# A second copy of the normalised tokens, ordered by remainder, for the values of two attention groups

## The reference

```
h = rmsnorm(x, mix_pre_norm)
z = h @ w_in
qa, ka, va, ... = split(z)
for g, (window, dil) in enumerate(((128, 1), (512, 4), (2048, 16))):
    o, lse = dilated_group_attention(qa[:, :, g], ka[:, :, g], va[:, :, g], bias[:, g], window, dil)
```

## Time and profile before

| | |
|---|---|
| median of 3 runs | 1440.94 us (1440.66 to 1441.42) |
| profiled execution | 1441.15 us, span in the trace 1439.0 us |
| granted TensorE clock | 0.999 of 2.4 GHz over the span |
| PE busy | 1431.7 us (99%) |
| PEld busy | 1227.9 us (85%) |
| DVE, ACT, POOL busy | 903.7 us (63%), 669.4 us (47%), 23.3 us (2%) |
| values, second and third group | from 376.93 to 424.12 us of the span |

### The profile page before, as it was taken

How to read it: one execution, slowest core, us unless ns; L and a number is a source line. 1 busy time by engine, 2 the same in 40 slices (tenths; PEclk the granted TensorE clock), 3 DMA queues, 4 the chain that set the end, 5 groups by cost and what they waited for, 6 DMA issues and landing times.

```text
span 1439.0 us, 21208 instructions
## 1 busy us (share of the span) xinstructions
PE 1431.7 (99%) x8104; PEld 1227.9 (85%) x8104; DVE 903.7 (63%) x1424; ACT 669.4 (47%) x1083; POOL 23.3 (2%) x43
## 2 busy tenths in 40 slices
PE   9999999999999999999999999999999999999998
PEld 8899999888898888888888888888889888888886
DVE  7888875335753455567866766664548555564975
ACT  5455555334532546555446554553445333233542
POOL 0000000000100000000000000000000000000000
PEclk9999999999999999999999999999999999999999
DMA  5333223324333323225322122224331243324653
GB/s 198 118 118 114 93 89 118 132 90 130 96 110 89 92 74 89 63 74 169 115 97 74 59 87 63 69 72 129 106 103 45 88 148 101 97 92 143 218 182 130
DMA packets 44317, 153.71 MB, mean 107 GB/s; under 512 B 5287, under 2 KB 5287, under 8 KB 44240
## 3 DMA queue, kind: packets, MB, share of 16 engines
q1 hardware_dynamic: 41472, 143.67, 31.3%
q0 software_dynamic: 2624, 8.95, 2.0%
q10 hardware_dynamic: 144, 0.04, 0.0%
HBM read 147.63 MB, written 4.23 MB: 106 GB/s over the span
## 4 chain that ended last, share of the span: by engine, by line
PE 98%; ACT 1%; DVE 1%; issue 0%; DVEq 0%; ACTq 0%
PE ps L470 21%; PE ps L471 21%; PE ps L472 21%; PE ps L637 4%; PE ps L638 4%; PE ps L639 4%; PE ps L1701 3%; PE ps L1700 3%; PE ps L1702 3%; PE ps L2530 1%; PE ps L2100 1%; PE ps L2101 1%; PE ps L2102 1%; PE ps L2913 1%; PE ps L2510 1%; PE ps L2933 1%
## 5 line engine op out<-in xcount | busy, mean ns | idle before, releaser
L470 PE MATMUL ps<-hh,whi 128*128 128x512 f32 x960 | 379.2, 395 | 0.1
L472 PE MATMUL ps<-hh,wlo 128*128 128x512 f32 x960 | 374.0, 390 | 0.0
L471 PE MATMUL ps<-hl,whi 128*128 128x512 f32 x960 | 373.9, 389 | 0.0
L416 DVE TENSOR_TENSOR wlo<-raw,whi 128x1024 fp32r<-128x1024 f32 x172 | 210.5, 1224 | 250.4 <-ACT whi L411 250.3
L411 ACT ACTIVATE whi<-raw 128x1024 fp32r<-128x1024 f32 x172 | 181.8, 1057 | 380.9 <-PE ps L472 356.3
L470 PEld LDWEIGHTS ps<-hh,whi 128*128 128x128 f32 x960 | 180.1, 188 | 42.6 <-issue 3.2
L472 PEld LDWEIGHTS ps<-hh,wlo 128*128 128x128 f32 x960 | 180.2, 188 | 38.1
L471 PEld LDWEIGHTS ps<-hl,whi 128*128 128x128 f32 x960 | 180.3, 188 | 35.7
L470 PE MATMUL ps<-ah,whi 128*128 128x512 f32 (+1 forms) x192 | 71.5, 372 | 0.0
L472 PE MATMUL ps<-ah,wlo 128*128 128x512 f32 (+1 forms) x192 | 71.3, 371 | 0.0
L471 PE MATMUL ps<-al,whi 128*128 128x512 f32 (+1 forms) x192 | 71.3, 371 | 0.0
(11 more groups left out here) (576 smaller groups left out, 3007.4 us busy)
## 6 DMA issues: line engine op xcount, KB each, us to landing
raw<-in_wstream SPq DMA_DIRECT2D x189, 512.0 KB, 3.5
w_raw<-in_wstream SPq DMA_DIRECT2D x32, 512.0 KB, 4.3
ring<-in_wstream SPq DMA_DIRECT2D x20, 512.0 KB, 4.3
xt<-in_x_t SPq DMA_DIRECT2D x16, 256.0 KB, 4.3
raw_early<-in_wstream SPq DMA_DIRECT2D x8, 512.0 KB, 4.4
raw_late<-in_wstream SPq DMA_DIRECT2D x4, 512.0 KB, 3.9
x_dram<-x_tok POOLq DMA_DIRECT2D x4, 512.0 KB, 4.1
x_tok<-x_dram POOLq DMA_DIRECT2D x4, 512.0 KB, 5.8
```

The lines of the kernel that those rows point to most:

```text
L416: nc.vector.tensor_tensor(wlo[:, s, :], raw[:, s, :], whi[:, s, :].bitcast(F32), ALU.subtract).then_inc(split_done, 1)
L470: nc.tensor.matmul(out, w, m, start=start, stop=False)
L471: nc.tensor.matmul(out, w, ml, start=False, stop=False)
L472: return nc.tensor.matmul(out, wl, m, start=False, stop=stop)
```

## The change

The change gives the second and third groups a stationary operand whose elements lie side by side.

- Sixteen new tiles, `hp_high0` to `7` and `hp_low0` to `7`, each [128, 4, 128]: the tokens of one `kt`, sorted by remainder. They lie in places that are used by others at other times: six of the high parts and the last two in the places of the attention's first `q_t` and `k_t`, the low parts where `whi_v` was and where `ath` and `atl` come later.
- POOL fills them for the second group: eight copies of `hh`, each when its tile is complete in both halves, then eight of `hl`, once PE is done with `whi_v`. PE waits for them tile by tile in the second group (`h_turned`).
- The normalised tokens are written straight into these tiles: DVE's `h_norm` reads `xt` and `rstd` in the order of the remainders and writes `tmp` in that order, ACT and DVE fill `hp_high` and `hp_low` from it.
- Later stages need the tokens' own order, so POOL copies each finished normalised tile back into `hh` and `hl`: 16 copies, after the bias transfers of the first two head pairs and ahead of the shift of the values. PE waits for all of them before the attention.
- Three transfers at the start count on one semaphore (`tables_in`) in place of two, so that ACT's wait at `table_h` and PE's waits for the constants are now for all three.

```
+        by_rest = "p (u r) -> p r u"
+        at[0] = arena + 51 * 1024
+        hp_high = [place(f"hp_high{i}", [P, R, U], F32R) for i in range(6)]
+        at[0] = arena + 68 * 1024
+        hp_high += [place(f"hp_high{i}", [P, R, U], F32R) for i in range(6, KT)]
+        at[0] = arena + 4 * S * (2 * FT + 1) + 4 * (2 * VEC + 3 * 32)
+        hp_low = [place(f"hp_low{i}", [P, R, U], F32R) for i in range(KT)]
...
-                        if t == 0 and g == 2:
-                            pe.wait_ge(sem("h_low"), IN_H + kt + 1)
+                        if t == 0:
+                            pe.wait_ge(*((sem("h_turned"), KT + kt + 1) if g == 1 else (sem("h_low"), IN_H + kt + 1)))
...
-                        m = [x[:, kt, :].rearrange("p (u r) -> p r u", r=R)[:, t, :] for x in (hh, hl)]
+                        m = hp_high[kt][:, t, :], hp_low[kt][:, t, :]
...
-                nc.scalar.activation(hh[:, d, :], tmp[:, d % 2, :], ACT.Copy).then_inc(sem("h_high"), 1)
+                nc.scalar.activation(hp_high[d][:].rearrange("p r u -> p (r u)"), tmp[:, d % 2, :], ACT.Copy
+                                     ).then_inc(sem("h_high"), 1)
...
-                nc.vector.scalar_tensor_tensor(out=tmp[:, d % 2, :], in0=xt[:, d, :], scalar=PRE2[:, d:d + 1],
-                                               in1=rstd[:], op0=ALU.mult, op1=ALU.mult).then_inc(sem("h_norm"), 1)
+                nc.vector.scalar_tensor_tensor(out=tmp[:, d % 2, :].rearrange("p (r u) -> p r u", r=R),
+                                               in0=xt[:, d, :].rearrange(by_rest, r=R), scalar=PRE2[:, d:d + 1],
+                                               in1=rstd[:].rearrange(by_rest, r=R), op0=ALU.mult, op1=ALU.mult
+                                               ).then_inc(sem("h_norm"), 1)
...
-                nc.vector.tensor_tensor(hl[:, d, :], tmp[:, d % 2, :], hh[:, d, :].bitcast(F32),
-                                        ALU.subtract).then_inc(sem("h_low"), 1)
+                nc.vector.tensor_tensor(hp_low[d][:].rearrange("p r u -> p (r u)"), tmp[:, d % 2, :],
+                                        hp_high[d][:].rearrange("p r u -> p (r u)").bitcast(F32), ALU.subtract
+                                        ).then_inc(sem("h_low"), 1)
...
+            for kt in range(KT):
+                pool.wait_ge(*counted("pre2", "ready", KT + kt + 1))
+                nc.gpsimd.tensor_copy(hp_high[kt][:], hh[:, kt, :].rearrange(by_rest, r=R)).then_inc(sem("h_turned"), 1)
+            pool.wait_ge(block_done, 2 * FIRST["v"] + 2)
+            for kt in range(KT):
+                nc.gpsimd.tensor_copy(hp_low[kt][:], hl[:, kt, :].rearrange(by_rest, r=R)).then_inc(sem("h_turned"), 1)
             pool.wait_ge(sem("vec_out"), 2)
             pool.dma_start(vec_dram.ap(), vec_sb[:]).then_inc(sem("pool_stored"), 16)
...
                     if hp == 2:
-
+                        pool.wait_ge(sem("h_turned"), 2 * KT)
+                        for d in range(KT):
+                            pool.wait_ge(sem("h_low"), IN_H + d + 1)
+                            for x, turned in ((hh, hp_high[d]), (hl, hp_low[d])):
+                                nc.gpsimd.tensor_copy(x[:, d, :].rearrange(by_rest, r=R), turned[:]
+                                                      ).then_inc(sem("h_turned"), 1)
                         pool.wait_ge(sem("v_scaled"), R)
...
             v_pe(pe)
             pe.wait_ge(sem("v_out0"), 2 * N_GROUPS + 1)
-            pe.wait_ge(sem("cst_in"), 16)
+            pe.wait_ge(sem("tables_in"), 48)
+            pe.wait_ge(sem("h_turned"), 4 * KT)
             attn_pe(pe)
```

More of the change, by code:

```diff
@@ L3297, in _ @@
             pool.wait_ge(sem(f"place_in{KT - 1}"), 16)
-            pool.dma_start(table[0:BUCKETS, :], rel_bias).then_inc(sem("hot_in"), 16)
-            pool.dma_start(hot_sb[:], onehot).then_inc(sem("hot_in"), 16)
-            pool.dma_start(cst[:], consts).then_inc(sem("cst_in"), 16)
+            pool.dma_start(table[0:BUCKETS, :], rel_bias).then_inc(sem("tables_in"), 16)
+            pool.dma_start(hot_sb[:], onehot).then_inc(sem("tables_in"), 16)
+            pool.dma_start(cst[:], consts).then_inc(sem("tables_in"), 16)
+            for kt in range(KT):
[4 more added lines that the diff above has]
+                nc.gpsimd.tensor_copy(hp_low[kt][:], hl[:, kt, :].rearrange(by_rest, r=R)).then_inc(sem("h_turned"), 1)
             pool.wait_ge(sem("vec_out"), 2)
@@ L3372, in _ @@
             nc.scalar.activation(lb_e[:], lb_e[:], ACT.Exp).then_inc(sem("lb_exp"), 1)
-            act.wait_ge(sem("hot_in"), 32)
+            act.wait_ge(sem("tables_in"), 48)
             act.wait_ge(sem("filled"), 1)
```

## The result

| | before | with the change |
|---|---|---|
| median | 1441.10 us (1440.66 to 1441.42, 4 runs) | 1458.86 us (1458.51 to 1460.08, 4 runs) |
| span in the trace | 1439.0 us | 1457.0 us |

The change makes the kernel slower: 17.8 us, a ratio of 1.0124 with a 95% interval of 1.011 to 1.0138. The forecast was 1452, its range 1441 to 1460.

A forecast was written before the change was run, and what follows sets the result against it. PE, busy 1431.7 of 1439.0 us, was taken as the bound. From 1441.15: less 1.6 for steps, plus 4.4 (first group's second half), plus 8.5 (second group's) gives 1452.4, forecast 1452, range 1441 to 1460.

The forecast's parts named there:

- PE's steps: Values' second and third groups: 192 matmul steps fall from 234.9 ns to 232.4 to 226.7, gaining 1.6 us (0.5 to 1.6).
- second half of the first group, first low copy: Seven copies at 0.85 us make DVE's last tile 3.7 us late, the first low part 0.7 more: 4.4 us.
- second half of the second group: DVE's chain to the last bank: six strided norms 2.3, eight copies back 6.8, less 0.6 to spare: 8.5 us.
- What bounds: PE, busy 1431.7 of 1439.0 us, bounds the kernel; time is won only by shorter steps, lost by PE waiting.
- One copy: A strided POOL copy takes 1.0 us, between 0.61 and 1.11; beside DVE it was priced at 0.85 us.
- rival 2: A POOL copy holds DVE for its whole length, 1.0 us each: 1456 us in all; chance 20%.
- Norms: DVE's `h_norm` reads both operands with the stride, 0.38 us more each; six on the chain, 2.3 us.
- At nothing: Bias transfers, shifted values, shared semaphore, PE's added waits and copies back ending before the attention at 424.12 cost nothing.
- No exclusion: Rival 1: copies and DVE run side by side, not slower: 1442.0 us, or 1439.6 with free norms; chance 24%.
- POOL was not the bound: Rival 3: POOL is the bound at 2.0 us a copy, some 1451 us, over 1460 with exclusion; chance 6%.

The follow-up runs named there:

- the run with the gain alone: Kernel before, but PE takes 128 neighbouring tokens as operand in the values' second and third groups: 1439.93 us, ratio 0.9991.
- the run with PE kept busy: Change without the first 16 copies, plus 27 matmuls with unread results queued on PE ahead of the third group: 1448.96 us, ratio 1.0052.
- with constants: Change with constants written by GpSimd memsets in place of the first 16 copies: 1448.08 us (one run).

## Why the prediction was right in direction and too small

The sum was 11.3 us; 17.95 us are in the trace. Term by term (PE's steps are what the group rows of the table of starts leave after the half clock; 192 steps by 3.5 ns would be 0.7):

| term | forecast | in the trace |
|---|---|---|
| PE's steps | -1.6 | -0.9 |
| second half of the first group, first low copy | 4.4 | 5.05 |
| stop at the second group's third bank | not listed | 3.1 |
| second half of the second group | 8.5 | 6.9 |
| half clock after the waits | not listed | 3.8 |

- *What bounds, and the direction.* Right. PE is the bound and loses by waiting; the gain is about what a measurement can tell.
- *PE's steps.* The mechanism was right, the size wrong. "I take 1.6, because 226.7 is the step of the plain matmuls that stand undisturbed": the run with the gain alone has that step, the new tiles have 231.4. The other end of my own bounds, 232.4, was nearer.
- *One copy.* I took 1.0 between 0.61 and 1.11. Undisturbed records are 1.11 to 1.12, the upper end. What a copy takes from DVE is 0.82 in the first group, where I took 0.85; in the second it is less (below).
- *The second half of the first group.* Right: the last matmul is 3.5 late (379.10 against 375.58), 3.7 forecast. The second group then begins another 1.5 later instead of 0.7. The profile names no releaser, but the first low copy ends at 381.88, 0.1 before PE begins: it and the last high copy were each held by a weight split, which rival 2 had and the forecast halved.
- *The stop at 386.72.* The step that failed. I followed the delay to PE's first matmul of the second group and stopped there. The copies of the first group's banks 2 and 3 stand on DVE behind the splits and three sums, each of them longer beside the low copies, and the sums' squares come from ACT in turn. They ran at 377.14 before, 385.39 after. Moving them shows it.
- *The second half of the second group.* Norms 2.3 by the runs and 2.3 forecast. The copies were priced too high: from the first norm to DVE's bank copies the chain takes 16.9 us (400.69 to 417.62) and took 9.65 before (391.18 to 400.83), 7.3 more, so the eight copies cost it 5.0 instead of 6.8, some 0.6 each. Here the copies follow each other without a gap and are themselves held, 1.5 to 2.0 us long; why one then takes less from DVE was not tried. I also took the wrong banks for PE's next need: it meets ACT's first, which come behind the third pair of norms and had 0.3 us to spare (they had left at 401.22, PE began at 401.49). Up to there it is 4.6 us of the 6.9, where the forecast had 6.8 of 8.5 (after the 0.6).
- *Half clock.* Not in the sum at all. Each wait was priced at its length. In the change the wait before the third group costs 2.3 more than its length, and without the first copies 2.5, which the run with PE kept busy wins back.
- *At nothing.* Right: the copies back end at 430.3, 11.7 us before the attention at 442.07, and no wait for the bias or the shifted values stands on PE.
- *Rivals.* No exclusion is refuted by every run with copies. Rival 2 said 1456; holding until the copy is over is right as a mechanism (the plain copies), though not at a whole microsecond a copy, and the time is beyond both for the two unlisted terms. POOL was not the bound: it stood idle for 4.15 us before the first copy back.
- *Luck.* The range held 1458.9 because its upper end had been set above rival 2. Of the three large misses two, the stop and the half clock, added 6.9 us that nobody had counted, and the high price of the copies back took 1.6 from them.

## What to carry to other kernels

Ask of every copy given to an idle GpSimd which DVE instructions run beside it: with two inputs in SBUF they stand still until the copy is over (a tensor-scalar was slowed too), a plain copy out of PSUM doesn't, and a write without a read slowed none. When a delay is priced, follow it past the first place where the bound engine waits to everything queued behind it on the slowed engine, and add to a long wait of PE the half clock that comes after it. And before paying for a shorter load, measure the step: loads 121 ns shorter made it 8 ns shorter at best.

## What the runs showed of the hardware that I had not expected

- The clock falls to its lower level in or behind a wait and stays there for a while: after waits of 4.5 to 6.8 us before the third group the next six to twelve matmuls start 0.43 us apart (the change, the runs without first copies, with plain copies, with constants, with the bank copies moved). After one of 2.1 to 2.4 us there (no copy, no copies back, copies back later) none did.
- The step of a matmul with short loads differs with the places of its operands: with the same weights 226.7 ns from `hh` and `hl` and 231.4 from the new tiles, and from `hh` and `hl` 226.7 with `whi_u` and 232.4 with `whi_v`.
- A GpSimd copy with 16 bytes between elements on one side takes 1.11 us, the plain one 0.61: nearly twice.
- The exclusion goes both ways: copies of 1.11 us were recorded with up to 2.07 us when DVE was ahead.
